# Adaptive-norm modulation partly as TensorE sums, another order in the opening, and token-wise norms in the gated attention

## The reference

```python
mod   = silu(c)     @ w_ada + b_ada          # 1024 -> 6144, of which the first 2048 matter first
mod_c = silu(c_ctx) @ w_ada + b_ada
h  = modulate(rms_norm(x_lat, norm1_g), sh1, sc1)      # h * (1 + scale) + shift
hc = modulate(rms_norm(x_ctx, norm1_g), sh1c, sc1c)
# token_mixer: latent and context projections of h and hc, then
k_nope, v = mla_keys_values(kv_c, kv_norm_g, w_ukv)    # rms_norm over 256 features, then @ w_ukv
q = heads(rms_norm(q_c, q_norm_g) @ w_uq, 8)           # rms_norm over 384 features
o_mla = attention(q_nope, q_rope, [k_nope, k_nope_c], [k_rope, k_rope_c], [v, v_c])
o_gla = gla_bidirectional(...)                         # 4 heads of 128, chunks of 64, both directions
y = rms_norm(o_gla, gla_norm_g) * silu(r)              # a norm over the 128 features of each head
```

## Time and profile before

| what | value |
| --- | --- |
| median of 3 runs | 3144.71 us (3144.42 to 3145.18) |
| the profiled execution's own time | 3140.14 us |
| its span, first to last instruction | 3138.1 us |
| mean granted clock of TensorE | 0.988 |
| TensorE busy | 3035.6 us, 97% |
| VectorE busy | 1426.4 us, 45% |
| ScalarE busy | 684.1 us, 22% |
| GpSimd busy | 2064.9 us, 66% |

### The profile page before, as it was taken

One profiled execution on the slowest core, in us unless ns is written; L12 is line 12 of the kernel. 1 busy time (PEld: TensorE's weight loads), 2 busy tenths in 40 slices (PEclk: granted clock), 3 DMA queues, 4 the chain that ended last, 5 costly groups with the idle time before them and its releaser, 6 DMA issues.

```text
span 3138.1 us, 38618 instructions
## 1 busy us (share of the span) xinstructions
PE 3035.6 (97%) x13632; PEld 2470.7 (79%) x13632; DVE 1426.4 (45%) x1857; ACT 684.1 (22%) x1191; POOL 2064.9 (66%) x2056
## 2 busy tenths in 40 slices
PE   5899999899999999999999999999999999999998
PEld 3777668778887788888888888888888887888886
DVE  7878742377456664222335322255422246442222
ACT  3244751111002532111122111100211115421110
POOL 4632227666666677777767777777777776777774
PEclk8999999999999999999999999999999999999999
DMA  6611112222222222222322222222222222322221
GB/s 257 234 56 34 41 61 95 87 88 99 96 95 93 94 101 98 97 94 100 107 81 94 98 97 94 100 94 95 100 94 99 96 94 94 103 99 94 100 95 67
DMA packets 86170, 307.24 MB, mean 98 GB/s; under 512 B 9569, under 2 KB 10081, under 8 KB 85793
## 3 DMA queue, kind: packets, MB, share of 16 engines
q1 hardware_dynamic: 82512, 297.73, 27.7%
q10 hardware_dynamic: 3536, 7.80, 0.7%
HBM read 303.39 MB, written 2.10 MB: 97 GB/s over the span
## 4 chain that ended last, share of the span: by engine, by line
PE 89%; DVE 7%; ACT 2%; SPq 1%; issue 1%; DMA 1%; ACTq 0%; DVEq 0%
PE acc L1601 85%; PE acc L732 1%; DVE rec_rec_x L2024 1%; PE side L759 1%; DVE ada_more L1170 1%; SPq L537 1%; DMA xc<-in_ctx 1%; PE side L742 0%; DVE state L1310 0%; PE side L1601 0%; PE stat L1664 0%; DVE n_scaled L1147 0%; PE acc L653 0%; DVE rec_rec_x L2022 0%; DVE att_stat L1372 0%
## 5 line engine op out<-in xcount | busy, mean ns | idle before, releaser
L1563 POOL TENSOR_TENSOR w_lo<-w_raw,w_hi 128x512 fp32r<-128x512 f32 x513 | 669.8, 1306 | 1005.1 <-PE acc L1601 974.9
L1601 PE MATMUL acc<-h_hi,w_hi 128*128 128x512 f32 x2224 | 875.6, 394 | 29.2 <-ACT gq L875 11.6
L1601 PE MATMUL acc<-h_hi,w_lo 128*128 128x512 f32 x2224 | 868.1, 390 | 0.0
L1601 PE MATMUL acc<-h_lo,w_hi 128*128 128x512 f32 x2224 | 868.1, 390 | 0.0
L1564 POOL TENSOR_TENSOR w_lo<-w_raw,w_hi 128x512 fp32r<-128x512 f32 x513 | 708.9, 1382 | 0.0
L1601 PEld LDWEIGHTS acc<-h_hi,w_hi 128*128 128x128 f32 x2224 | 418.8, 188 | 129.8 <-issue 15.0
L1601 PEld LDWEIGHTS acc<-h_hi,w_lo 128*128 128x128 f32 x2224 | 419.1, 188 | 85.2
L1601 PEld LDWEIGHTS acc<-h_lo,w_hi 128*128 128x128 f32 x2224 | 419.2, 188 | 85.0 <-issue 1.9
L1552 POOL TENSOR_SCALAR w_hi<-w_raw 128x512 fp32r<-128x512 f32 x513 | 404.0, 787 | 37.3 <-DMA w_raw<-in_weights 37.3
L1993 DVE TENSOR_TENSOR x<-acc,x 128x512 f32 (+1 forms) x160 | 110.7, 692 | 661.8 <-PE acc L1601 661.7
L1601 PE MATMUL acc<-mlp_hid_hi,w_hi 128*128 128x512 f32 x1024 | 398.3, 389 | 0.0
(11 more groups left out here) (350 smaller groups left out, 3535.4 us busy)
## 6 DMA issues: line engine op xcount, KB each, us to landing
w_raw<-in_weights SPq DMA_DIRECT2D x513, 512.0 KB, 3.2
ada<-in_ada SPq DMA_DIRECT2D x36, 512.0 KB, 5.6
ada_more<-in_ada SPq DMA_DIRECT2D x10, 512.0 KB, 18.3
x<-in_x ACTq DMA_DIRECT2D x16, 256.0 KB, 6.8
out<-x SPq DMA_DIRECT2D x8, 256.0 KB, 2.2
cvec<-in_cvec ACTq DMA_DIRECT2D x1, 1024.0 KB, 6.0
ada_n<-in_ada SPq DMA_DIRECT2D x2, 512.0 KB, 17.4
xc<-in_ctx SPq DMA_DIRECT2D x1, 1024.0 KB, 16.7
```

The costliest lines, as they stand in the source:

```text
L1563: pool.tensor_tensor(w_lo[:, slot, 0:half], w_raw[:, slot, 0:half], w_hi[:, slot, 0:half].bitcast(F32), ALU.subtract)
L1601: ins = pe.matmul(out, lhs, rhs, start=start, stop=stop, skip_group_check=group)
```

## The change

Four of the 16 modulation tiles stay with VectorE (`ADA_ROWS`). The other 12 go to TensorE: with the tile as the stationary operand and the two vectors as two columns, eight matmuls of 2 columns sum one tile for both vectors (`ada_rows`, L611 of the changed kernel), and the result stands in a free part of `side`. The tiles are loaded in the order of `ADA_ORDER`, behind the whole of `cvec` and of `x`, with panels 0 and 1 between. The squares of `x` are added by GpSimd, and TensorE sums them over the partitions with one matmul (L647), which stands after the fifth of its twelve tiles. VectorE multiplies `x` in place by the inverse root before gains are known (L1244), then applies gain and shift in one operation of its own (L1250), so ScalarE makes only `h_hi`. TensorE runs the first two projections side by side, the second two tiles behind (`first_two`). The context's square sums come behind the third projection, from squares kept for all eight tiles, and what is left of the context's norm follows behind.

For the norms of queries, of keys and of the gated heads, squares are the stationary operand and `ones` the moving one, so a sum has its tokens on the partitions (`token_sums`, and `sum` in the loop). ScalarE takes the root and VectorE the inverse of a 128x4 result instead of 128x512. ScalarE writes the inverses on a diagonal by scaling an identity matrix (`head_diagonal`, `key_diagonal`), and TensorE spreads them to all partitions with `ones` (`spread` at each odd step, `keys` once). VectorE multiplies output, gain and gate with the spread values. The keys' scaling moves behind the gated loop. In the key pairs, ScalarE keeps the latent's bank and VectorE copies the context's.

The diff, cut to its core:

```diff
+ADA_ROWS = 4
+ADA_ORDER = [4, 0, 5, 6, 1, 7, 8, 2, 9, 10, 3, 11, 12, 13, 14, 15]
+ADA_ORDER_PE = [m for m in ADA_ORDER if m >= ADA_ROWS]
+SECOND_LAG = 2
...
+            sp.dma_start(x[:, 0:KT // 2, :], io["x"][:, 0:KT // 2, :]).then_inc(x_in, 16)
+            for m in ADA_ORDER[:-2]:
                 load_ada(m)
+            load_panel(sp, 0, 0)
+            for m in ADA_ORDER[-2:]:
+                load_ada(m)
+            load_panel(sp, 1, 1)
             sp.dma_start(xc[:, :, :], io["ctx"]).then_inc(ctx_in, 16)
-            for n in range(SLOTS):
+            for n in range(2, SLOTS):
...
+            def ada_rows(i):
+                m = ADA_ORDER_PE[i]
+                pe.wait_ge(ada_in[m], 16)
+                for j in range(KT):
+                    ins = pe.matmul(ada_columns[:, m - ADA_ROWS, :], ada_slot[m][:, P * j:P * j + P], c_cols[:, j, :],
+                                    start=(j == 0), stop=(j == KT - 1))
+                if i == len(ADA_ORDER_PE) - 1:
+                    ins.then_inc(ada_sums, 1)
...
+            def first_two():
+                a, b = begin_out(), begin_out()
+                pe.wait_ge(panel_made, 1)
+                for k in range(KT + SECOND_LAG):
+                    if k < KT:
+                        cols = slice(P * k, P * k + P)
+                        pe.wait_ge(h_lo_made, k + 1)
+                        mm(a, w_hi[:, 0, cols], h_hi[:, k, :], k == 0, False)
+                        mm(a, w_hi[:, 0, cols], h_lo[:, k, :], False, False)
+                        ins = mm(a, w_lo[:, 0, cols], h_hi[:, k, :], False, k == KT - 1)
+                        if k == KT - 1:
+                            ins.then_inc(out_made, 1)
+                    j = k - SECOND_LAG
+                    if j == 0:
+                        pe.wait_ge(panel_made, 2)
+                    if j >= 0:
+                        cols = slice(P * j, P * j + P)
+                        ins = mm(b, w_hi[:, 1, cols], h_hi[:, j, :], j == 0, False)
+                        if j == KT - 1:
+                            ins.then_inc(panel_used, 1)
+                        mm(b, w_hi[:, 1, cols], h_lo[:, j, :], False, False)
+                        ins = mm(b, w_lo[:, 1, cols], h_hi[:, j, :], False, j == KT - 1)
+                ins.then_inc(out_made, 1)
+                tile[0] += 2 * TP
...
+            for i in range(len(ADA_ORDER_PE)):
+                ada_rows(i)
+                if i == 4:
+                    pe.wait_ge(summed, KT)
+                    pe.matmul(stat[:, :], ones[:, :], square_sum[:, :], start=True, stop=True).then_inc(first_stat, 1)
+            first_two()
+            project(h_parts)
+            pe.wait_ge(root_made, 1)
+            for k in range(KT):
+                pe.wait_ge(squared, KT + k + 1)
+                pe.matmul(stat[:, 0:C], ones[:, :], ctx_squares[:, k, :], start=(k == 0), stop=(k == KT - 1)).then_inc(summed, 1)
+            for _ in AHEAD:
...
+                for b in range(n):
+                    for k in range(tiles):
+                        ins = pe.matmul(out[:, P * b:P * b + P], low_square[:, at(k, b):at(k, b) + P], ones[:, :],
+                                        start=(k == 0), stop=(k == tiles - 1))
                 ins.then_inc(out_made, 1)
+            token_sums(QL, 4, lambda k, b: T * k + P * b)
+            token_sums(KVL, 4, lambda k, b: QL * T + TC * k + P * b)
+            token_sums(KVL, KB - 4, lambda k, b: QL * T + TC * k + T + P * b)
...
                 if name == "sum":
                     pe.wait_ge(gla_sq, i + 1)
                     out = begin_out()
+                    for b in range(4):
+                        ins = pe.matmul(out[:, P * b:P * b + P], square[:, i % 2, P * b:P * b + P], ones[:, :], start=True, stop=True)
+                    ins.then_inc(out_made, 1)
+                if name == "spread":
+                    pe.wait_ge(head_diag, i + 1)
+                    out = begin_out()
                     pe.matmul(out[:, :], ones[:, :], square[:, i % 2, :], start=True, stop=True).then_inc(out_made, 1)
+                if name == "keys":
+                    pe.wait_ge(key_diag, 1)
+                    for c0, c1 in ((0, T), (T, TC)):
+                        out = begin_out()
+                        pe.matmul(out[:, 0:c1 - c0], ones[:, :], key_spread[:, c0:c1], start=True, stop=True)\
+                          .then_inc(out_made, 1)
...
+            def head_diagonal(h):
+                act.wait_ge(head_inverse, h + 1)
+                for b in range(4):
+                    ins = act.activation(square[:, h % 2, P * b:P * b + P], identity[:, :], ACT.Copy, scale=head_rstd[:, 1, b:b + 1])
+                ins.then_inc(head_diag, 1)
+            def key_diagonal():
+                act.wait_ge(low_inverse, 1)
+                for b in range(KB):
+                    ins = act.activation(key_spread[:, P * b:P * b + P], identity[:, :], ACT.Copy, scale=low_rstd[:, 4 + b:5 + b])
+                ins.then_inc(key_diag, 1)
...
+                o = OUT_KH + 2 * pair
+                wait_made(act, o)
+                act.activation(k_t[0:64, 2 * pair, 0:T], bank(o)[0:64, :], ACT.Copy)
+                act.activation(k_t[0:64, 2 * pair + 1, 0:T], bank(o)[64:P, :], ACT.Copy).then_inc(out_taken[o % BANKS], 1)
+            head_diagonal(GH - 1)
...
+            def normed(norm, src, k):
+                own(dve.tensor_tensor(src[:, k, :], src[:, k, :], rstd[:, 0:sums(norm)], ALU.mult), normed_made, KT * norm + k + 1)
+            def modulated(n0, src, hi, lo, s):
                 for k in range(KT + 1):
                     if k < KT:
-                        dve.tensor_tensor(scaled_[:, k % 2, 0:w], src[:, k, 0:w], rstd[:, 0:w], ALU.mult)\
-                           .then_inc(n_scaled_made, 1)
+                        own(dve.tensor_scalar(src[:, k, :], src[:, k, :], gain1[:, s, k:k + 1],
+                                              mod[:, k, s:s + 1], ALU.mult, ALU.add), n_scaled_made, n0 + k + 1)
                     if k:
                         dve.wait_ge(h_hi_made, n0 + k)
...
+            dve.wait_ge(silu_made, 2)
+            for m in range(ADA_ROWS):
                 ada_product(m, 0)
-            for m in range(ADA_FIRST - 2, ADA_FIRST):
                 ada_product(m, 1)
+            rstd_of(0)
+            for k in range(KT - 2):
+                normed(0, x, k)
             gains(0)
-            rstd_of(0)
-            modulated(0, 0, x, h_hi, h_lo, n_scaled, n_full)
-            for m in range(ADA_FIRST - 2):
-                ada_product(m, 1)
+            for k in range(KT - 2, KT):
+                normed(0, x, k)
+            modulated(0, x, h_hi, h_lo, 0)
...
+            def head_inverses(h):
+                wait_taken(dve, OUT_GLA["sum", h])
+                if h:
+                    dve.wait_ge(head_diag, h)
+                own(dve.reciprocal(head_rstd[:, 1, :], head_rstd[:, 0, :]), head_inverse, h + 1)
             def head_output(h):
 
-                wait_taken(dve, OUT_GLA["sum", h])
-                link(dve.reciprocal(root[:, :], root[:, :]))
+                o = OUT_GLA["spread", h]
                 wait_taken(dve, OUT_GLA["r", h])
-                dve.wait_ge(gla_o, 2 * h + 2)
-                link(dve.scalar_tensor_tensor(out=o_norm[:, :], in0=side[:, h % 2, :], scalar=col("gla_norm"),
-                                              in1=root[:, :], op0=ALU.mult, op1=ALU.mult))
-                own(dve.tensor_tensor(o_norm[:, :], o_norm[:, :], gr[:, h % 2, :], ALU.mult), gla_y, h + 1)
+                wait_made(dve, o)
+                if h:
+                    dve.wait_ge(og_hi_made, h)
+                take(dve.scalar_tensor_tensor(out=o_norm[:, :], in0=gr[:, h % 2, :], scalar=col("gla_norm"),
+                                              in1=bank(o), op0=ALU.mult, op1=ALU.mult), o)
+                own(dve.tensor_tensor(o_norm[:, :], side[:, h % 2, :], o_norm[:, :], ALU.mult), gla_y, h + 1)
...
+                o = OUT_KH + 2 * pair + 1
+                wait_made(dve, o)
+                dve.tensor_copy(k_t[0:64, 2 * pair, T:TC], bank(o)[0:64, 0:C])
+                take(dve.tensor_copy(k_t[0:64, 2 * pair + 1, T:TC], bank(o)[64:P, 0:C]), o)
+                if pair == 0:
+                    head_inverses(GH - 1)
...
+            if not start_x:
+                for k in range(1, KT):
+                    pool.wait_ge(squared, k + 1)
+                    if k == 1:
+                        pool.tensor_tensor(square_sum[:, :], square[:, 0, :], square[:, 1, :], ALU.add).then_inc(summed, 2)
+                    else:
+                        pool.wait_ge(summed, k)
+                        pool.tensor_tensor(square_sum[:, :], square_sum[:, :], square[:, k % 2, :], ALU.add).then_inc(summed, 1)
```

More of the change, by code:

```diff
@@ L111, in gla_order @@
     for u in range(GLA_STEPS):
+        if u % 2 == 1 and u > 1:
+            order.append(("spread", u // 2 - 1, 1))
         order += [("turned", u, 2), ("intra", u, 1), ("added", u, 1)]
```

(6 more changed lines are left out.)

218 lines of the change are left out of this document (110 added, 108 removed).

## The result

The change made the kernel slower by a little: the median of 20 runs is 3149.22 us (3146.68 to 3151.53) against 3144.71 us (3140.18 to 3146.05, 20 runs too), a ratio of 1.0017 with a 95% interval of 1.0010 to 1.0023. The forecast was 3135.3, so it was 13.9 us too low, outside its range, and on the wrong side. The profiled execution took 3146.94 us with a span of 3145.1, 7.0 more than that of before.

What follows compares the result with a forecast made beforehand. The prediction took TensorE, busy 3035.6 of 3138.1 us, as the bound. Opening -3.8, gated loop -12.2, keys and values +6.6 make -9.4 us, taken off the median: 3135.3 us, range 3122 to 3147 (forecast's own 3129 to 3141).

Steps and rivals of the forecast that it cites:

- The opening: Start of the kernel up to the first context projection: modulation tiles, norms and first projections, forecast to save 3.8 us.
- the mark: Start of the first context projection, counted as if at full speed: forecast to move from 102.5 to 98.7 us.
- the cover of 2 us: In the opening, the context's norm was to be hidden behind three projections with 2 us to spare.
- The narrow passes: TensorE's 2-column passes for the modulation tiles: lower clock level, 0.213 us a pass, 3.4 us a tile.
- Rival 1: In the opening, tiles run at the upper level or narrow passes cost 0.11 at either: 3124.6 us, chance 0.26.
- rival 2: The opening gives nothing, passes cost 0.256 us, so -3.8 becomes +4.4: total 3143.5 us, chance 0.17.
- The gated loop: Gated attention: fewer reciprocals, bank waits and low-clock stretches, less added spreads and sums, in all -12.2 us.
- Rival 3: In the gated loop, three spreads wait for ScalarE's diagonal, behind VectorE's inverse: +11 us, 3155.7 us, chance 0.12.
- Keys and values: Key pairs and last spread wait for VectorE's copies and ScalarE's diagonal, with low clock behind: +6.6 us.

Runs made afterwards that it cites:

- after_aligned: The changed kernel with 6 floats less of filling, so that the shift is 256 bytes: 3140.26 us, ratio to before 0.9989.
- ctx_early: after_aligned with the context's square sums ahead of the third projection instead of behind it: 3138.50 us, ratio to before 0.9980.
- keys_interleaved: after_aligned with VectorE's context key copies between the rotary copies, last head's inverse ahead of them, ScalarE's last diagonal behind the second key pair: 3134.73 us.
- rows6: after_aligned with six modulation tiles on VectorE and ten on TensorE, instead of four and twelve, by turns: 3134.75 us, ratio to before 0.9967.
- tiles_wide: after_aligned with one further wide matmul (two passes of 512 columns) behind each of the 12 modulation tiles: 3157.71 us, ratio to before 1.0043.

## Why the prediction was wrong

**The step that failed is one that the sum does not have.** The prediction priced instructions, transfers and waits, and took the allocation lines as nothing. They cost 9.0 us (3149.22 to 3140.26), and 32 bytes more in the kernel before cost 8.1 by themselves. With a shift of 256 bytes the change is faster, by 4.2 us. The prediction had named three signs of being wrong (tiles that end before 50, spreads that wait in the loop, key pairs that do not wait). None of them came, and the time was on the wrong side all the same, because all three look at instructions and none at the matmuls that the change leaves alone. The traces show how 0.0067 us becomes this: where two matmuls of 512 columns with weights of a panel start less than 0.245 us apart, the time over a pace of 0.2267 adds up to 8.7 us in the changed kernel, 1.8 in the kernel before and 1.7 in after_aligned. The rest of the 7.6 us between the spans of the changed kernel and of after_aligned is not split further. A part of it is that matmuls of 256 columns on the context's tiles, which have moved as well, are slower: 0.1202 apart between 110 and 165 us, against 0.1180 before and in after_aligned. Nothing in the trace of before could show the rule, since all its starts stand alike. What could have been seen is that the kernel has fillings in units of `LINE` at all, and that the change's filling no longer summed to that unit once each tensor is rounded up.

**The opening** was forecast at -3.8 and gives +1.1 (not to be told from nothing). In the trace the mark moves from 102.5 to 103.4, where the forecast said 98.7. The tiles, GpSimd's sum (28.9, forecast 30.4), the first h tile and the first two projections (74.5, forecast 75) were right. Three terms were not. The context's sums were put at 16 x 0.118, which is the spacing of the one-pass projections of 256 columns, and took 3.62: their fp32 passes start 0.216 apart. The earlier trace rows have fp32 passes of 512 columns (0.53 each, 1.06 for two); half of that, 0.265, would have been too much by less than 0.118 was too little. Because TensorE had gained 0.7 in the first two projections, its projections ended only 1.0 us late (99.66). VectorE's eight multiplications for the context took 0.82 instead of 0.45, with GpSimd's splits beside them for most of that time (5.1 of 6.6 us), its eight tiles behind them 1.17 instead of 1.0, and the last of them came at 101.7 instead of 97. So the cover of 2 us was gone, and a wait of 2.1 took its place. Behind it followed 1.65 us at the lower level, which I had left out although show the same behind the wait of before. 1.0 + 2.1 + 1.65 is the 4.7 between forecast and trace, and ctx_early took most of the wait away. The 1.65 is partly luck of the run: keys_interleaved has the same wait and no low stretch behind it. The prediction also left VectorE unused and did not say so: in the trace its products end at 31.2 and it stands 11.1 us until the tiles end at 57. rows6 turns part of that into 5.5 us.

**The narrow passes** were right for the right reason. The forecast took 0.213 at the lower level, as twice what it had for the upper; the trace has 0.213 (0.215 with the tail of the last), and tiles_wide shows both levels (0.213 and 0.112). Rival 1 (the upper level) falls, and rival 2 (0.256 a pass) too. Its 0.256 was a misreading of the earlier trace rows: the 2.05 us for eight passes hold a slow first one and the tail of the last, and the records between start 0.213 apart. The rule from the Trainium skill (TensorE: Matmul & The Clock Gate, section LDWEIGHTS) would give 0.107 us for 128 columns at either level. The trace is near that at the upper level (0.112 a pass) and not at the lower (0.213); the load records last 0.19 us at the one and 0.333 at the other.

**The gated loop** was forecast at -12.2. Between the first decay matmul (166.96, after_aligned 167.46) and the first query projection (311.32, after_aligned 301.22) it is -10.6. The bank waits and the low stretches went (10.7 to 0.6); new are two waits of 1.1 for the head's output in the state matmuls, 2.2 in all, more than the missing 1.6. They are not a steady number: in three of the experiments the level falls behind the second of them (ctx_early, rows6, keys_interleaved), and 1.8 to 3.0 us more go there. Rival 3, that spreads wait in the loop, did not come.

**Keys and values** were forecast at +6.6, with waits of 3.6 and about 2, and a low stretch. The traces have 3.5, 2.3 and a first matmul of 0.77 behind the wait; from the query projections to the scores after_aligned lies 7.0 us above before. keys_interleaved gave 5.5 of them back, which shows that the place of VectorE's copies and of the last diagonal is the cause.

**The sum.** Forecast -9.4, aligned -4.2, as built +4.5. Of the 13.9 us, 9.0 are the start addresses and about 5 the opening; the two terms of the gated half missed by 1.6 and 0.4 in the trace, and its median by 1.7. One more caution on the numbers: the profiled execution of before (3140.14) was as short as the shortest of its 20 runs (3140.18), so differences of spans come out larger against it than differences of medians.

## What to carry to other kernels

A change that adds a small tensor moves every tensor behind it. Before pricing instructions, compare the start addresses of the operands of the matmuls that fill the span, and keep them where they stood to each other; measure a suspicious loss by adding a filling to the kernel before. When work moves to an engine that had been idle, look at once for the other engine's new idle time, because the best split is rarely the one written down. And where a norm is hidden behind a fixed number of projections, price the path that is hidden with the rows of its engine when its neighbour is busy, and allow for a low-clock stretch behind any wait, as a range and not as a fixed term: the same wait had one in one run and none in another.

## What the runs showed of the hardware

- The pace of a matmul of 512 columns, with new weights each time, depends on how the start of the moving tensor stands to that of the weights. Moved by 0 or 256 bytes a partition: 0.2267 us; by 64: 0.2289; by 32, 128 or 288: 0.2333. Moving all together by 128 changes nothing. With matmuls of 256 columns between them the effect is there too (0.1202 against 0.1180 at 288, 0.1203 at 32). Other distances, and why, were not tried.
- At full clock this loss leaves no mark in TensorE's busy share (40.00 of 40 us in both windows), in waits or in the granted clock. Only the spacing, or the number of matmuls in a window, shows it.
- The granted clock reads 1.00 from the start of the program to its first recorded change, while TensorE can be at its lower level (starts 0.43 us apart at 62.25 and 62.68).
- Eighty passes of 2 columns, back to back for 17 us, did not raise the level (0.213 us apart from first to last). In tiles_wide, with one matmul of 512 columns in two passes after every tile, it rose once, for 3.4 us.
- A pass of 2 columns with 128 columns of new weights starts 0.112 us after the last at the upper level and 0.213 at the lower; an fp32 pass of 256 columns 0.216 at the upper.
- Whether the level falls behind a short wait differs from run to run of the same instructions: behind 2.06 us the granted clock of 102 to 106 was 0.57 in after_aligned and 1.00 in keys_interleaved; behind 1.10 us in the gated loop it stayed at 1.00 in after_aligned and fell to 0.70 (262 to 272) in ctx_early.
